# Attention of the first block: V products over four units, padded q and k, and the steps at the edges of the attention

## The chip, the cores and the metric

One core of a Trainium2 chip runs the whole program in one launch. The metric is the device time of a run in microseconds (us), as the median of several runs; lower is better.

## The reference, cut to what matters

The program computes two blocks one after the other on a sequence of 1024 positions with width 1024, in float32: the first block (two layers, l = 0 and 1), then a hybrid layer. Only the first block is touched.

```python
for l in range(2):
    h = rms_norm(x, norm_g[l]);  p = h @ w_in[l]
    c_q, c_kv, k_pe, z_a, u_f, z_f, g_a, g_f = split(p)
    q = rms_norm(rms_norm(c_q) @ w_uq)      # 8 heads of 96: 64 plain, 32 rotary
    k, v = ...                              # k: 8 heads of 96, v: 8 heads of 64
    rope(q[..., 64:]), rope(k[..., 64:])
    o_a = softmax(q @ k.T * 96 ** -0.5) @ v # 1024 x 1024 scores per head
    y_a = (o_a * silu(z_a)) @ w_attn_proj[l]
    y_f = (fourier(u_f) * silu(z_f)) @ w_fourier_proj[l]
    m = sigmoid(g_a + b0) * y_a + sigmoid(g_f + b1) * y_f
    x = x + m @ w_out[l]
```

## The kernel before, in words

Every engine runs a list of instructions written by hand, with semaphores between the engines. The eight PSUM banks (128 x 512 float32) are handed over by the counters `full[b]` (written by TensorE) and `free[b]` (read by the others); `begin(b)` waits for a bank, `arrive(b)` waits for its content.

**Attention.** A *unit* is one head and one tile of 128 queries: 64 units per layer, u = 8h + t. For a unit TensorE makes the scores (`scores`, L551: q and k are kept as a rounded part and a rest, so 3 products for each half of the 1024 keys, 6 matmuls of 512 columns, 96 rows deep), into the bank pair 0/1 or 2/3. VectorE takes the row maximum (L1712), ScalarE the exponential (L1295). TensorE turns the probabilities (`p_turn`, L561: 8 transposes of 128x128 into banks 4 and 5); VectorE copies both banks for an even unit (L1720, L1721), for an odd one VectorE copies bank 4 (L1725) and ScalarE bank 5 (L1288), into one of two buffers `PT`. `pv_pair` (L575) multiplies two turned units with V at once: V has 64 columns, so the even unit stands in the left column half of the array and the odd unit in the right one, 8 steps of keys with 128 columns moved for each. After eight units VectorE copies the head's output from bank 6 (`head_out`, L1687 and L1688).

On TensorE step u is: scores of u+1, for even u the V products of units u-2 and u-1, a turn of q or k for the next head if one is due (`qk_turn`, L535, four for each head, all through bank 7), the turn of unit u. GpSimd stages q and k of each head beforehand (L2174 to L2188). Each turned quarter is copied and rounded by ScalarE (`qk_copy`, L1271), and its rest is made by VectorE (`qk_rest`, L1695), which frees the bank. The four turns of head 0 go through bank 7 one after the other before the first scores.

**Around the last head.** In the last head's steps 1 to 4 ScalarE also rounds a quarter of h (`round_h`, L1275) and VectorE makes its rest (`rest_of_h`, L1700); a step later ScalarE rounds h in place (`in_place`, L1279). When the last head's output is copied, VectorE sets `s_o`. Then follow weights and rests 0 and 1, h parts 4 to 7 (ScalarE, VectorE; parts 6 and 7 in place by GpSimd, L2195), the turn of the row sums (L597) and its copy (L1323). Then TensorE runs *unit weights* c = 0 to 7 with n = 0, 1 (`unit`, L614, L617, L620: 24 matmuls of 512 columns each, over k = 0 to 7). Before it starts, ScalarE has rounded weight 0 into `wHi` (`round_weights`, L1311) and VectorE has its rest (`rest`, L1737).

**End of a layer.** For each m = 0 to 7 the gates (`unit`) and the two projections (L644), which VectorE multiplies and adds to `mT` (L1772, L1774). Then `m @ w_out` (L658, L661, L664) needs the rounded m (ScalarE L1356 and L1363), its rest (`m_rest`, L1779) and the rounded weights with their rest (L1360, `w_out_rest` L1785).

**SyncE's queue** loads the weights in chunks into two slots; a load waits for `w_used[slot]`. Slot 0's chunk "zf" (unit weights 0 to 3) waits for the first Fourier matmul; "za" in slot 1 waits for `s_o`.

## Time and profile before

| | us |
|---|---|
| median of 3 runs | 2679.63 (2676.92 to 2685.85) |
| the profiled execution's own time | 2685.18 |
| its span, first to last instruction | 2683.4 |
| TensorE busy | 2534.9 (94%) |
| VectorE busy | 1365.2 (51%) |
| ScalarE busy | 797.5 (30%) |
| GpSimd busy | 367.4 (14%) |
| mean granted TensorE clock | 0.974 of full |

PE is TensorE's matmuls, PEld its weight loads, DVE VectorE, ACT ScalarE, POOL GpSimd. The span is cut into stretches by time from its start; a granted clock of 1.00 is 2.4 GHz, 0.50 is 1.2 GHz. Attention of layer 0 runs from 212 to 459 us, of layer 1 from 1130 to 1377 us. A float32 matmul leaves two records, a float32 transpose and a rounded matmul one.

### The profile page before, as it was taken

How to read it: one execution, taken by the hardware profiler on the slowest of the kernel's cores; microseconds unless marked ns; L12 is line 12 of the kernel's file. 1: busy time of each engine (PE TensorE's matmuls, PEld its weight loads, DVE VectorE, ACT ScalarE, POOL GpSimd, SP SyncE). 2: the span in 40 equal slices, each digit the busy share in tenths (PEclk: the TensorE clock that was granted, in tenths of full speed). 3: DMA queues.
4: the chain of work that ended last, by engine and by line, in shares of the span. 5: the costliest groups of instructions: out<-in, count | busy, mean ns of one | idle time of the engine just before them, and what ended most of it. 6: DMA issues, size and time to landing. Idle time of an engine off the chain costs nothing.

```text
span 2683.4 us, 30039 instructions
## 1 busy us (share of the span) xinstructions
PE 2534.9 (94%) x12173; PEld 1776.7 (66%) x12173; DVE 1365.2 (51%) x2206; ACT 797.5 (30%) x1434; POOL 367.4 (14%) x477
## 2 busy tenths in 40 slices
PE   7998997999999999899979999999999998989997
PEld 5856886876666787588868666667556544445553
DVE  2255776221113243467753111133689999955763
ACT  3343545111113142345441111131351113143341
POOL 0023320000000001233100000000234672100000
PEclk9998999999999999999989999999999999999998
DMA  5010000211113121000020111122111011020000
GB/s 197 29 47 1 1 1 32 58 47 42 30 47 126 35 93 44 32 1 1 1 64 24 48 47 47 55 94 69 66 39 34 1 41 40 32 71 24 32 16 32
DMA packets 106377, 116.78 MB, mean 44 GB/s; under 512 B 20704, under 2 KB 78784, under 8 KB 106240
## 3 DMA queue, kind: packets, MB, share of 16 engines
q1 hardware_dynamic: 105088, 110.66, 13.4%
q10 hardware_dynamic: 1152, 4.19, 0.4%
q8 instruction: 97, 1.59, 0.2%
q14 instruction: 40, 0.33, 0.0%
HBM read 96.82 MB, written 16.84 MB: 42 GB/s over the span
## 4 chain that ended last, share of the span: by engine, by line
PE 84%; DVE 8%; ACT 4%; issue 1%; POOL 1%; SPq 1%; DMA 1%; DVEq 0%; POOLq 0%; ACTq 0%
PE PS L644 8%; PE PS L614 7%; PE PS L617 7%; PE PS L620 7%; PE PS L551 6%; PE PS L445 4%; PE PS L561 4%; PE PS L575 4%; PE PS L969 4%; PE PS L735 4%; PE PS L882 2%; PE PS L658 2%; PE PS L661 2%; PE PS L664 2%; PE PS L940 2%; PE PS L490 2%
## 5 line engine op out<-in xcount | busy, mean ns | idle before, releaser
L614 PE MATMUL PS<-hHi,R2bR 128*128 128x512 f32 x768 | 306.7, 399 | 15.4 <-ACT rows L1323 15.4
L617 PE MATMUL PS<-hLo,R2bR 128*128 128x512 f32 x768 | 300.5, 391 | 0.0
L620 PE MATMUL PS<-hHi,R2bR 128*128 128x512 f32 x768 | 300.2, 391 | 0.0
L1737 DVE TENSOR_TENSOR R2bR<-W,R2bR 128x1024 fp32r<-128x1024 f32 x48 | 57.5, 1222 | 309.2 <-ACT R2bR L1311 309.2
L1343 ACT ACTIVATE R3a<-PS,pT 128x512 f32<-128x512 f32 x64 | 42.3, 687 | 467.5 <-PE PS L620 467.5
L614 PEld LDWEIGHTS PS<-hHi,R2bR 128*128 128x128 f32 x768 | 145.2, 189 | 48.9 <-ACT rows L1323 15.7
L1712 DVE TENSOR_REDUCE negm<-PS 128x1 f32<-128x1024 f32 x128 | 156.6, 1223 | 29.8 <-PE PS L551 25.1
L617 PEld LDWEIGHTS PS<-hLo,R2bR 128*128 128x128 f32 x768 | 145.3, 189 | 33.0 <-issue 3.3
L735 PE MATMUL PS<-hT,W 128*128 128x512 f32 x384 | 166.6, 595 | 0.0
L1295 ACT ACTIVATE R2b<-PS,negm 128x1024 f32<-128x1024 f32 x128 | 142.4, 1112 | 78.8 <-DVE negm L1712 78.8
L620 PEld LDWEIGHTS PS<-hHi,R2bR 128*128 128x128 f32 x768 | 145.2, 189 | 30.5
L561 PE MATMUL PS<-ident,R2b 128*128 128x128 f32 x1024 | 138.6, 279 | 5.6 <-ACT R2b L1295 3.8
L2012 DVE MAX8 ssc<-R2a 128x8 f32<-128x384 f32 (+4 forms) x160 | 132.4, 828 | 5.4
L575 PE MATMUL PS<-R2b,R 128*64 128x128 f32 x2048 | 129.1, 280 | 6.4 <-DVE R2b L1725 3.1
L575 PEld LDWEIGHTS PS<-R2b,R 128*64 128x64 f32 x2048 | 113.7, 139 | 29.5 <-issue 22.3
L735 PEld LDWEIGHTS PS<-hT,W 128*128 128x128 f32 x384 | 72.9, 191 | 91.0 <-issue 90.9
L2013 DVE MATCH_REPLACE8 R2a<-ssc,R2a 128x384 f32<-128x384 f32 (+4 forms) x160 | 129.4, 809 | 0.0
L561 PEld LDWEIGHTS PS<-ident,R2b 128*128 128x128 f32 x1024 | 113.8, 142 | 20.8 <-issue 13.1
L1772 DVE TENSOR_TENSOR R3a<-R3a,PS 128x512 f32<-128x512 f32 x64 | 43.8, 684 | 162.7 <-PE PS L644 162.7
L445 PE MATMUL PS<-W,hT 128*128 128x256 f32 (+1 forms) x512 | 119.8, 393 | 0.9 <-DMA W<-in_w_in 0.7
L969 PE MATMUL PS<-W,R 128*128 128x512 f32 x256 | 117.2, 603 | 0.8 <-DVE R L2060 0.8
L551 PE MATMUL PS<-R3aR 96*128 96x512 f32 x256 | 114.8, 448 | 3.1 <-DVE WR L1695 3.1
(354 smaller groups left out, 4645.8 us busy)
## 6 DMA issues: line engine op xcount, KB each, us to landing
W<-in_w_in SPq DMA_DIRECT2D x10, 2048.0 KB, 8.5
W<-in_w_in SPq DMA_DIRECT2D x33, 512.0 KB, 4.7
xres<-R SPq DMA_DIRECT2D x3, 4096.0 KB, 18.7
W<-in_w_out SPq DMA_DIRECT2D x6, 2048.0 KB, 7.9
R<-xres SPq DMA_DIRECT2D x2, 4096.0 KB, 19.0
R<-in_x ACTq DMA_DIRECT2D x8, 512.0 KB, 8.2
W<-in_w_in SPq DMA_DIRECT2D x4, 1024.0 KB, 6.8
R3a<-rsums SPq DMA_DIRECT2D x16, 256.0 KB, 5.4
```

Source lines behind the costliest of these rows:

```text
L445: mm = pe.matmul(o[:, 0:hi - lo], hT[:, k, t * P:(t + 1) * P], wc[:, k, lo:hi], start=(k == 0), stop=(k == 7))
L551: mm = pe.matmul(PS[:, b + n, :], x[0:QK, t * P:(t + 1) * P], y[0:QK, n * 512:(n + 1) * 512], start=(i == 0), stop=(i == 2))
L561: mm = pe.transpose(o[:, k * P:(k + 1) * P], Pb[u % 2][:, c * P:(c + 1) * P], ident[:, :])
L575: mm = pe.matmul(PS[e * VD:(e + 1) * VD, 6, at_], v_tok[:, k, h, :], PT[e][:, k * P:(k + 1) * P], start=(k == 0), stop=(k == 7))
L614: mm = pe.matmul(o, wHi[c % 2][:, k, :], hHi[:, k, ns], start=(k == 0), stop=False)
L617: mm = pe.matmul(o, wHi[c % 2][:, k, :], hLo[:, k, ns], start=False, stop=False)
L620: mm = pe.matmul(o, wLo[c % 2][:, k, :], hHi[:, k, ns], start=False, stop=(k == 7))
L644: mm = pe.matmul(o, g[:, k0 + k, :], rhs[:, k, n * 512:(n + 1) * 512], start=(k == 0), stop=(k == 3))
L735: mm = pe.matmul(o, wz[:, k, m * P:(m + 1) * P], xT[:, k, n * 512:(n + 1) * 512], start=(k == 0), stop=(k == 7))
L969: mm = pe.matmul(o, mix[:, k, t * P:(t + 1) * P], wo[:, k, :], start=(k == 0), stop=(k == 7))
L1295: act.activation(Pb[u % 2], PS[:, b:b + 2, :].rearrange("p a c -> p (a c)"), ACT.Exp, bias=negm[:, u:u + 1], accum_out=rsum[:, u:u + 1]).t ...
L1712: dve.tensor_reduce(negm[:, u:u + 1], PS[:, b:b + 2, :].rearrange("p a c -> p (a c)"), AX.X, ALU.max, negate=True).then_inc(s_nm, 1)
```

## The change

1. V products of four units at once (`pv_quad`): each column half takes two units, 256 columns moved. Eight key steps, cut into pieces of 3, 3 and 2 in TensorE's steps 4q+4, 4q+5, 4q+6; the last quad in one piece.
2. Six buffers `PT` (three pairs): one pair as before, two in weight slot 0, and for the last head's units in the place of `q_tok`. Slot 0 is now given to "zf" by the V product that ends head 6; copies for the last head wait for `s_stage`.
3. q and k padded from 96 to 128 columns with zeros (a memset by GpSimd), so turns, copies and scores use 128 rows.
4. The four turns of head 0 use banks 4, 5, 6, 7.
5. `head_out` moves from step 1 to step 3 of the next head.
6. Around the last head: weight 0 is rounded in step 63, its rest comes before the last `head_out`; unit 0 starts right after the last V product, k = 0 to 3 for both n first, then k = 4 to 7; the row sums are turned behind it, into bank 7, and copied after ScalarE's second SiLU.
7. End of a layer: `m_rest` and `w_out_rest` of k = 0, 1 come before VectorE's multiplications of m = 7.

```diff
+def turn_bank(h, i):
+    return 4 + i if h == 0 else 7
...
-        PT = [R2b[:, 2, :], R2b[:, 3, :]]
+        def PT_pair(u):
+            i = u // 2 % 3
+            if i == 0:
+                return R2b[:, 2:4, :]
+            home = W[:, 0, 0:4096] if u < UNITS - NT else r0[:, 0:4096]
+            return home[:, (i - 1) * 2048:i * 2048].rearrange("p (a c) -> p a c", a=2)
+        def PT(u):
+            return PT_pair(u)[:, u % 2, :]
...
                 def scores(u):
...
                     if t == 0:
-                        pe.wait_ge(free[7], bk.count(7))
+                        for i in range(4):
+                            if h == 0 or i == 3:
+                                pe.wait_ge(free[4 + i], bk.count(4 + i))
...
-                            mm = pe.matmul(PS[:, b + n, :], x[0:QK, t * P:(t + 1) * P],
-                                           y[0:QK, n * 512:(n + 1) * 512], start=(i == 0), stop=(i == 2))
+                            mm = pe.matmul(PS[:, b + n, :], x[:, t * P:(t + 1) * P],
+                                           y[:, n * 512:(n + 1) * 512], start=(i == 0), stop=(i == 2))
...
+                def pv_quad(q, part):
+                    h, a_ = q // 2, q % 2
+                    if part[0] == 0:
+                        if a_ == 0:
+                            begin(6)
+                        pe.wait_ge(free[4], pt_count[4 * q + 3][0])
+                        pe.wait_ge(free[5], pt_count[4 * q + 3][1])
+                    for k in part:
+                        for e in range(2):
+                            mm = pe.matmul(PS[e * VD:(e + 1) * VD, 6, 2 * a_ * P:2 * (a_ + 1) * P], v_tok[:, k, h, :],
+                                           PT_pair(4 * q + 2 * e)[:, :, k * P:(k + 1) * P],
+                                           start=(k == 0), stop=(k == 7))
+                            if (h, a_, k, e) == (H - 2, 1, NT - 1, 0):
+                                mm.then_inc(w_used[0], 1)
...
-                    if u >= 2 and u % 2 == 0:
-                        pv_pair(u - 1)
+                    if u == UNITS:
+                        pv_quad(u // 4 - 1, range(NT))
+                    elif u >= 4 and u % 4 < 3:
+                        pv_quad(u // 4 - 1, range(3 * (u % 4), min(NT, 3 * (u % 4) + 3)))
...
-                pe.wait_ge(s_o, l + 1)
-                o = begin(0)
-                pe.transpose(o[:, 0:P], sums[:, :], ident[:, :]).then_inc(full[0], 1)
...
-                for c in range(8):
+                o = [begin(0), begin(1)]
+                for n in range(2):
+                    unit(0, n, o[n], None, range(KD // 2))
+                for n in range(2):
+                    unit(0, n, o[n], None, range(KD // 2, KD)).then_inc(full[n], 1)
+                pe.wait_ge(s_o, l + 1)
+                o = begin(7)
+                pe.transpose(o[:, 0:P], sums[:, :], ident[:, :]).then_inc(full[7], 1)
+                for c in range(1, 8):
...
@@ ScalarE @@
+                    if u == UNITS - 1:
+                        act.wait_ge(full[5], bk.count(5))
+                        round_weights(0)
...
+                for k in range(4, KD):
+                    round_h(k)
+                in_place(4)
                 act.wait_ge(s_o, l + 1)
...
                 round_weights(1)
...
+                in_place(5)
...
@@ VectorE @@
+                dve.wait_ge(full[5], bk.count(5))
                 rest(0)
...
+                head_out(H - 1)
+                dve.wait_ge(free[6], bk.count(6))
+                dve.memset(mark[:, :], 0.0).then_inc(s_o, 1)
+                for k in range(4, KD):
+                    rest_of_h(k)
                 rest(1)
...
                 for m in range(KD):
                     if m + 1 < KD:
                         rest(8 + 2 * m + 2)
                         rest(8 + 2 * m + 3)
+                    else:
+                        for k in range(2):
+                            m_rest(k)
+                            w_out_rest(k)
...
@@ GpSimd @@
+                pool.memset(stage[:, :, :, QK:P], 0.0)
```

The order of the instructions before and after, at three places. First TensorE in the middle of the attention, from the turn of an even unit on, before (L551 scores, L561 turn of probabilities, L575 V products, L535 turn of q or k):

```order
L561 MATMUL PS<-ident,R2b 128x128 x8
L551 MATMUL PS<-R3aR 128x512
L551 MATMUL PS<-WR,R3aR 128x512
L551 MATMUL PS<-R3aR,WR 128x512
L551 MATMUL PS<-R3aR 128x512
L551 MATMUL PS<-WR,R3aR 128x512
L551 MATMUL PS<-R3aR,WR 128x512
L535 MATMUL PS<-ident,R 96x128 x4
L561 MATMUL PS<-ident,R2b 128x128 x8
```

and in the changed kernel the first piece of a quad, with the turn behind it (L566 scores, L576 turn of probabilities, L590 V products):

```order
L566 MATMUL PS<-R3aR,WR 128x512
L590 MATMUL PS<-R2b,R 64x256
L590 MATMUL PS<-W,R 64x256
L590 MATMUL PS<-R2b,R 64x256
L590 MATMUL PS<-W,R 64x256
L590 MATMUL PS<-R2b,R 64x256
L590 MATMUL PS<-W,R 64x256
L576 MATMUL PS<-ident,R2b 128x128 x8
```

Where one group of 16 matmuls of 128 columns stood in every second step, groups of 6, 6 and 4 matmuls of 256 columns stand in three of four steps. Second, VectorE at the end of the attention (L1737 rest of a unit weight, L1700 rest of h, L1732 the mark that sets `s_o`), before:

```order
L1725 COPY R2b<-PS 128x512
L1684 RECIPROCAL sums<-sums 128x8
L1687 COPY R2a<-PS 64x4x128
L1688 COPY R2a<-PS 64x4x128
L1732 MEMSET mark 128x1
L1737 TENSOR_TENSOR R2bR<-W,R2bR 128x1024
L1700 TENSOR_TENSOR hLo<-hT,R3aR 128x1024 x2
L1737 TENSOR_TENSOR R2bR<-W,R2bR 128x1024
L1700 TENSOR_TENSOR hLo<-hT,R3aR 128x1024 x2
```

and after:

```order
L1754 COPY R2b<-PS 128x512
L1762 TENSOR_TENSOR R2bR<-W,R2bR 128x1024
L1710 RECIPROCAL sums<-sums 128x8
L1713 COPY R2a<-PS 64x2x256
L1714 COPY R2a<-PS 64x2x256
L1768 MEMSET mark 128x1
L1727 TENSOR_TENSOR hLo<-hT,R3aR 128x1024 x4
L1762 TENSOR_TENSOR R2bR<-W,R2bR 128x1024
```

The rest of weight 0 now stands ahead of the last head's output. Third, VectorE at the end of a layer (L1790 is `m_rest`, L1796 `w_out_rest`, L1813 and L1815 the multiplications and the addition), after:

```order
L1790 TENSOR_TENSOR hHi<-R,R3aR 128x1024
L1796 TENSOR_TENSOR R2bR<-W,R2bR 128x512
L1790 TENSOR_TENSOR hHi<-R,R3aR 128x1024
L1796 TENSOR_TENSOR R2bR<-W,R2bR 128x512
L1813 TENSOR_TENSOR R3a<-R3a,PS 128x512 x2
L1815 TENSOR_TENSOR R<-R3a 128x512
L1813 TENSOR_TENSOR R3a<-R3a,PS 128x512 x2
L1815 TENSOR_TENSOR R<-R3a 128x512
```

Before, the first four of these stood behind the last four.

## Rows read from the trace of the kernel before

**Rows 1.** The page: TensorE's busy time, and the chain by engine.
```profile
PE 2534.9 (94%) x12173; PEld 1776.7 (66%) x12173; DVE 1365.2 (51%) x2206; ACT 797.5 (30%) x1434; POOL 367.4 (14%) x477
...
PE 84%; DVE 8%; ACT 4%; issue 1%; POOL 1%; SPq 1%; DMA 1%; DVEq 0%; POOLq 0%; ACTq 0%
```

**Rows 2.** Stretches: length, busy (records) of PE, PEld, DVE, ACT, POOL; PEclk, DMA, GB/s.
```profile
212.20:222.30 10.10, 3.80 (x17) 2.35 (x17) 2.75 (x4) 3.29 (x5) 6.43 (x9) 0.59 0.00 0
222.30:231.20 8.90, 8.90 (x24) 6.89 (x25) 3.74 (x4) 2.77 (x5) 2.39 (x3) 0.50 0.01 2
231.30:424.30 193.00, 192.29 (x1751) 163.91 (x1749) 143.87 (x183) 96.12 (x165) 53.56 (x66) 1.00 0.01 1
459.40:468.90 9.50, 0.33 (x1) 0.14 (x1) 8.23 (x9) 7.96 (x9) 0.98 (x1) 0.70 0.63 221
469.00:473.50 4.50, 4.50 (x11) 3.53 (x12) 0.00 (x0) 1.28 (x1) 4.50 (x2) 0.50 0.31 92
842.50:846.30 3.80, 0.00 (x0) 0.01 (x1) 3.11 (x4) 1.13 (x2) 0.00 (x0) 0.91 0.00 0
846.40:852.40 6.00, 6.00 (x14) 4.68 (x15) 3.66 (x4) 4.45 (x6) 0.00 (x0) 0.50 0.63 230
```

**Rows 3.** The chain in the steady attention (start, length in us, what).
```profile
300.69 1.02 PE PS L561 x8
...
303.54 0.87 PE PS L561 x8
304.41 1.38 PE PS L551 x6
305.79 1.90 PE PS L575 x32
```

**Rows 4.** The chain from the Fourier matmuls through head 0's turns.
```profile
209.36 0.88 PE PS L526 x4
...
212.10 0.14 issue
...
214.42 1.07 PE PS L535 x4
...
215.51 0.60 ACT R3aR L1271
...
216.21 0.70 DVE WR L1695
...
222.29 0.77 PE PS L551
```

**Rows 5.** The chain in the last head, one step of 5.53 us.
```profile
435.66 1.15 DVE negm L1712
...
441.19 1.15 DVE negm L1712
```

**Rows 6.** Timeline around the end of the attention: VectorE, GpSimd.
```profile
459.36 0.69 DVE L1687 COPY R2a<-PS 64x512 f32<-64x512 f32 x1 [2.48 <-PE PS L575]
466.62 2.35 DVE L1700 TENSOR_TENSOR hLo<-hT,R3aR 128x1024 fp32r<-128x1024 f32 x2
467.92 5.60 POOL L2195 TENSOR_TENSOR hHi<-hT,hLo 128x1024 fp32r<-128x1024 f32 x2 [77.16 <-DVE hLo L1700]
```

**Rows 7.** Timeline, TensorE: start of unit 1, and the 42nd matmul behind it.
```profile
482.09 0.39 PE L614 MATMUL PS<-hHi,R2bR 128*128 128x512 f32 x1
...
491.61 0.39 PE L614 MATMUL PS<-hHi,R2bR 128*128 128x512 f32 x1
```

**Rows 8.** Timeline, end of the layer: rounding of m, its first rest.
```profile
829.35 1.05 ACT L1356 ACTIVATE R3aR<-R 128x1024 fp32r<-128x1024 f32 x1
839.16 0.69 DVE L1772 TENSOR_TENSOR R3a<-R3a,PS 128x512 f32<-128x512 f32 x1 [6.21 <-PE PS L644]
843.92 1.22 DVE L1779 TENSOR_TENSOR hHi<-R,R3aR 128x1024 fp32r<-128x1024 f32 x1
```

**Rows 9.** Issues of DMAs, 455 to 600 us: size, time to landing.
```profile
W<-in_w_in SPq DMA_DIRECT2D x1, 2048.0 KB, 8.2
```

More of the change, by code:

```diff
@@ L531, in qk_turn @@
                     pe.wait_ge(s_stage, l * 2 * H + 2 * h + i // 2 + 1)
-                    o = begin(7)
+                    b = turn_bank(h, i)
+                    o = begin(b)
                     for j in range(4):
                         t = 4 * (i % 2) + j
-                        mm = pe.transpose(o[0:QK, j * P:(j + 1) * P], stage[:, i // 2, t, :], ident[:, :])
+                        mm = pe.transpose(o[:, j * P:(j + 1) * P], stage[:, i // 2, t, :], ident[:, :])
                         if h == i == j == 0:
                             mm.then_inc(w_used[1], 1)
-                    mm.then_inc(full[7], 1)
+                    mm.then_inc(full[b], 1)
                 def scores(u):
@@ L563, in p_turn @@
                     pt_count.append((bk.count(4), bk.count(5)))
-                def pv_pair(u):
-                    h, t = u // NT, u % NT
-                    if t == 1:
-                        begin(6)
-                    pe.wait_ge(free[4], pt_count[u][0])
-                    pe.wait_ge(free[5], pt_count[u][1])
-                    at_ = slice((t // 2) * P, (t // 2 + 1) * P)
-                    for k in range(NT):
-                        for e in range(2):
-                            mm = pe.matmul(PS[e * VD:(e + 1) * VD, 6, at_], v_tok[:, k, h, :],
-                                           PT[e][:, k * P:(k + 1) * P], start=(k == 0), stop=(k == 7))
-                    if t == NT - 1:
+                def pv_quad(q, part):
[6 more added lines that the diff above has]
+                    for k in part:
+                        for e in range(2):
+                            mm = pe.matmul(PS[e * VD:(e + 1) * VD, 6, 2 * a_ * P:2 * (a_ + 1) * P], v_tok[:, k, h, :],
[3 more added lines that the diff above has]
+                                mm.then_inc(w_used[0], 1)
+                    if a_ == 1 and part[-1] == NT - 1:
                         mm.then_inc(full[6], 1)
@@ L592, in _, with unit @@
                         p_turn(u)
-                pe.wait_ge(s_o, l + 1)
-                o = begin(0)
-                pe.transpose(o[:, 0:P], sums[:, :], ident[:, :]).then_inc(full[0], 1)
                 def follows(c):
                     return 0 < c <= 8 or c % 2 == 1
-                def unit(c, n, o, last_used=None):
+                def unit(c, n, o, last_used=None, part=range(KD)):
                     ns = slice(n * 512, (n + 1) * 512)
-                    if n == 0:
+                    if n == part[0] == 0:
                         pe.wait_ge(s_wlo, l * N_SPLIT + c + 1)
-                    for k in range(KD):
+                    for k in part:
                         if c == n == 0:
@@ L1334, in _ @@
                         round_weights(i // 2 + 2)
+                    if i == 1:
+                        o = arrive(7)
+                        act.activation(rsT, o[UNITS:P, 0:P], ACT.Copy).then_inc(free[7], 1)
+                        act.wait_ge(s_hlo, l * KD + KD)
+                        act.wait_ge(free[7], bk.count(7))
+                        act.sem_inc(s_rsT, 1)
                 for m in range(KD):
@@ L1724, in _ @@
                             o = arrive(4)
[L1725 removed]
+                            dve.tensor_copy(PT(u - 1)[:, 0:512], o).then_inc(free[4], 1)
                     if u - 1 in QK_TURNS:
@@ L1729, in _ @@
                         rest_of_h(u % NT - 1)
-                head_out(H - 1)
-                dve.wait_ge(free[6], bk.count(6))
-                dve.memset(mark[:, :], 0.0).then_inc(s_o, 1)
                 def rest(c):
@@ L2171, in _ @@
                     rk = rsh[:, 1, :, h:h + 1]
-                    if h >= 1:
+                    if h == 1:
+                        pool.wait_ge(full[4], bk.count(4))
+                        pool.wait_ge(full[5], bk.count(5))
+                    elif h >= 2:
                         pool.wait_ge(full[7], bk.count(7) - 2)
@@ L2181, in _ @@
                     pool.tensor_tensor(x2p, rtp[:, 2], rtp[:, 3], ALU.add).then_inc(s_stage, 1)
+                    if h == 1:
+                        pool.wait_ge(full[6], bk.count(6))
                     if h >= 1:
@@ L2189, in _ @@
                                        ).then_inc(s_stage, 1)
-                    for _ in range(4):
-                        bk.take(7)
+                    for i in range(4):
+                        bk.take(turn_bank(h, i))
                 for k in range(H_ACT, KD):
@@ L2198, in _ @@
                     if b != 7:
-                        bk.n[b] += n
+                        bk.n[b] += n - (b > 3)
+                bk.take(7)
                 for n in ROUND[7:]:
```

86 lines of the change are left out of this document (36 added, 50 removed).

## The prediction

> **What bounds the kernel now.** I read the page first: TensorE is busy for 94% of the span and makes 84% of the chain that ended last [rows 1]. So a change pays where it shortens TensorE's stream, fills its idle stretches, or brings its clock back. The busy time by stretches says where that can be [rows 2]. In the steady attention (231.3 to 424.3 us) TensorE is busy for 192.29 of 193.0 us at clock 1.00: only its own work counts there. Four stretches of layer 0 are different. In 212.2 to 222.3 it is busy for 3.8 of 10.1 us, and 222.3 to 231.2 runs wholly at clock 0.50. In 459.4 to 468.9 it does next to nothing, and 469.0 to 473.5 runs at 0.50. In 842.5 to 846.3 it does nothing, and 846.4 to 852.4 runs at 0.50. Layer 1's chain has the same pieces with the same lengths, 918 us later. The chains and timelines show what ends each wait.
>
> **Part by part, for one layer.** I count gains as positive.
>
> *Turns of head 0 in four banks.* Now each turn waits until VectorE has taken the rest of the one before: turn 1.07, copy 0.60, rest 0.70 and latencies make a round of 2.62 us [rows 4], four of them from 212.24 to 222.29. TensorE is free at 210.24, when the last Fourier matmul ends, and VectorE frees the last Fourier bank (7) at 212.10 [rows 4]. Banks 4 to 6 are free earlier, so three turns run from 210.3 on and the fourth at 212.24, where the first stands now. Its copy ends near 213.5. VectorE is the last: four rests of 0.6 to 0.7 from 212.1 on end near 214.6, and the scores start near 214.7 instead of 222.29. **+7.6.** It can't be much less (four rests in line is all that is left) nor more (bank 7): 6.8 to 7.8. GpSimd may stage head 1 from about 211.3 on; its memset of the padding comes before head 0's staging, which is done 10 us before the first turn, so it costs nothing.
>
> *Clock at the start.* After work became dense at 222.3 the clock stayed at 0.50 for 8.9 us; at the two other places dense work got it back after 4.6 us and 6.1 us [rows 2]. I expect it to fall again (TensorE has about 2 us of idle before the scores), and to come back after some 6 to 7 us: half of the 2 us fewer, **+1.0**, between 0 (the same 8.9 us) and 2.2 (4.6 us).
>
> *V products.* Two units of 128 columns take 1.90 us [rows 3]. A transpose moves 128 columns in 0.87/8 = 0.109 us [rows 3], and 16 pairs of V records, the halves side by side, would take 16 x 0.109 = 1.74. So the columns already stream at full rate in both halves, and 0.16 us is paid on entering. Behind them the 8 transposes take 1.02 instead of 0.87 [rows 3]: another 0.15 on leaving. A group of V products therefore costs 0.31 us beside its columns. 256 columns take 0.88/4 = 0.22 (by L526) [rows 4], so a quad streams in about 3.47 us against 3.49 for two pairs: nothing. But a quad has three groups where two pairs had two. Per layer there are 15 x 3 + 1 = 46 groups instead of 32, 14 more, 4.3 us. Not all of it is paid. Through heads 1 to 6 it is: 12 quads x (0.31 - 0.02) = 3.5 us. The first quad starts two steps later than the first pair, so the last head begins with one pair (2.05 with its edges) owed. In the last head the steps 57 to 60 take 5.53 us each [rows 5], set by a loop over VectorE (rest of h, maximum) and ScalarE (exponential, two roundings), which TensorE waits for; a group more is hidden there. At the end the last quad is whole, 3.78 in place of 2.05, and the group at step 62 is shorter (1.18 for 2.05); `head_out` goes out of the loop into a wait of VectorE in step 59, which gives back little, since TensorE's group at step 57 stands there. Sum: the last V product ends 3.5 - 2.05 + 1.73 - 0.87 = 2.3 later, less a few tenths for `head_out`: **-2.0**, between -1 and -4.3.
>
> The Trainium skill (TensorEngine Tiling (Array Packing), Key Properties) says that changing the tiling mode drains the engine, which speaks against cutting a quad into three. The row above agrees with it (0.31 us beside the columns), and by it every one of the 14 groups would pay.
>
> *Padding.* Six score matmuls of 96 rows take 1.38 us [rows 3]; unit matmuls of 128 rows take (491.61 - 482.09)/42 = 0.227 us, 1.36 for six [rows 7]. If the 0.02 us is the 96 rows, 64 units give up to 1.5 us a layer; if it is the entry from the transposes, nothing. **+0.7**, 0 to 1.5.
>
> The Trainium skill (TensorE: Matmul & The Clock Gate, "Why this matters for your kernels") has a matmul with few rows take as long as one with 128; by that this term is 0 and the total 44.0 instead of 45.4.
>
> *End of the attention.* Now VectorE's copy behind TensorE's last V product starts at 459.36; two copies, the mark, weight 0, four roundings and the turn of the sums stand between it and unit 0 at 468.9, which runs at 0.50 to 473.5 and ends where unit 1 begins, 482.09 [rows 2, 6, 7]: 22.7 us. In the new order weight 0 is rounded in step 63 and its rest follows, both before the last V product, so unit 0 starts at once (T'). Parts k = 0 to 3 for both n take 24 x 0.227 = 5.45 us. Meanwhile VectorE copies the output (2 x 0.69), marks (T' + 1.5), and makes four rests, 2.35 for two [rows 6]: parts 4 to 7 at T' + 2.7, 3.8, 5.0, 6.1. ScalarE follows for 4 and 5. GpSimd needs 2.8 us each for 6 and 7 [rows 6]: T' + 7.8 and 10.6. TensorE wants part 6 at T' + 6.8 and part 7 at 7.5, so it waits about 3 us in all, finishes n = 0 at 11.3 and n = 1 at 14.0; the turn of the sums adds 0.2. **+8.5** (22.7 - 14.2), between 6.5 (GpSimd slower beside VectorE, or the clock falling in the wait) and 11 (no wait at all: 22.7 - 10.9 - 0.2 = 11.6).
>
> What is queued there: on ScalarE step 63's weight stands before the copy of bank 5, for which the last V product waits; it fits into the wait for that turn. It also needs chunk "zf", which SyncE now issues only after step 58's V product (near 432 in today's trace) and which lands 8.2 us later [rows 9]; it is wanted near 454, so 14 us are left. Behind it on SyncE stand only loads that wait for `s_o` anyway. The sums go to DRAM some 17 us behind T' instead of 10, and are first multiplied in at 521.
>
> *End of the layer.* VectorE now starts the first rest of m at 843.92, after all of m = 7, though ScalarE had rounded m at 829.35 to 830.4 [rows 8]. In the new order the four moved operations (two of 1.23, two of 0.69) and ScalarE's part run from 830.4 to about 836, before the projection that ends the wait of 6.21 us at 839.16 [rows 8], so the multiplications aren't late. TensorE goes on at 842.5 instead of 846.3: 3.8 us [rows 2]; and without that gap the clock should not fall, which gives back half of 6.1 us. **+6.9**, between 4 (the clock falls nevertheless) and 7. Parts 2 to 7 follow every 3.3 us, TensorE needs 5.45 for each.
>
> **Sum**: 7.6 + 1.0 - 2.0 + 0.7 + 8.5 + 6.9 = 22.7 us a layer, 45.4 for two. The profiled execution took 2685.18 us, 5.5 above the median, so it would take 2639.8; against the median of 2679.63 it is 2634.2. The ends of the terms give 2 x 13.0 = 26 and 2 x 28.5 = 57 us, thus 2623 to 2654.
>
> **The rivals.**
>
> *The clock stays low (chance 0.10).* Dense work from 214.7 on could run at 0.50 until 231.2 as now, 16.5 us instead of 8.9, which costs 3.8; and the 3 us wait in unit 0 could make the clock fall, for 4.5 us as at 469 [rows 2], which costs 2.3. With the 1.0 not gained: 7.1 us a layer, 2648. For it: the clock fell at all three gaps. Against it: TensorE works before and after these waits, and does so for much less than half of them now.
>
> *VectorE becomes late in the attention (0.07).* The shortest step (no V products) has 1.38 + 0.44 + 0.87 = 2.7 us of TensorE, and with `head_out` VectorE has 1.15 + 1.6 + 1.2 = 3.9 in it. If the delay isn't caught up in the next, longer steps, each head loses about 1 us, 14 in all: 2648. Against it: VectorE is busy for only 143.87 of 193 us [rows 2].
>
> *The two column halves don't overlap with 256 columns (0.05).* The moved operand is now a two-piece pattern over two buffers, in two memory regions. If the halves ran one after the other, each of the 64 pairs of units would stream for 3.49 instead of 1.74 us: +112 us, 2746, slower than before. The change comes out slower from the point where 45.4/112 = 41% of the overlap is lost. Against it: the two records of a pair start side by side now, also from different buffers, which is why 32 take 1.90 us [rows 3].
>
> *More than forecast (0.06).* No fall of the clock at the start (3 more), no wait in unit 0 (3), full padding gain (0.8): 6.8 a layer, 2620.
>
> **How the numbers follow.** The forecast has 0.72 and is 2634. With the first, second and last rival near its ends, 2619 to 2653 leaves out less than 2 in 10. About 0.3% (8 us) is what a measurement of this kernel can tell from no change. Faster by more: forecast, clock, late VectorE, the better case and a sliver of the third rival, 0.94. Within it 0.02. Slower 0.04.
>
> **What would show it.** Right: first scores 2.5 us behind the last Fourier matmul's VectorE operations; the V products in groups of about 1.3, 1.3 and 0.87 us with 0.3 beside them, and 28.5 instead of 28.0 us for a head; unit 0 directly behind the last V product, GpSimd the releaser of a 2 to 3 us wait within it; w_out directly behind the projections at clock 1.00. Wrong: V groups of 2.6 us; a wait for ScalarE's weight 0 or for its DMA; VectorE as releaser of TensorE in the steady steps; clock 0.50 for more than 9 us behind the first scores.

## The result, and the profile after

| | before | changed |
|---|---|---|
| median of four runs, us | 2679.60 (2676.92 to 2685.85) | 2647.86 (2641.66 to 2649.50) |
| the profiled execution's own time | 2685.18 | 2641.66 |
| its span | 2683.4 | 2639.6 |
| mean granted TensorE clock | 0.974 | 0.988 |

The changed kernel is faster: the ratio of the mean times is 0.9874, with an interval of 0.985 to 0.9898, and the medians differ by 31.7 us. The forecast was 45.4. A second set of runs of the changed kernel (e14, below) has a median of 2645.92 and the same ratio, 0.9874 (0.9861 to 0.9888).

The two profiled executions lie at opposite ends: the one of before is 5.5 us above its median, the one of after 6.2 below. So the spans differ by 43.8 us where the medians differ by 31.7, and a sum over the spans has to be cut into stages. The *touched stages* reach from the end of the first Fourier part to the end of the first block. They took 1645.2 us before, 1606.4 after, and 1609.2 in the profile of the second set, whose execution (2649.58) lies above its median, as that of before does. The change is thus worth 36.0 to 38.8 us in its own stages, and 36.0 where two executions at like ends are compared. The rest of the difference between the spans lies in code that the change doesn't touch. The kernel before reached the end of the Fourier part 1.8 us sooner (210.2 us against 212.0), and took 6.8 us more behind the first block, where the clock's spells (stretches in which it is at 0.50) lie elsewhere.

The page of the changed kernel, for [rows 1]: busy times, and the chain by engine.

```profile
PE 2519.7 (95%) x11149; PEld 1714.2 (65%) x11149; DVE 1368.2 (52%) x2206; ACT 797.1 (30%) x1434; POOL 370.1 (14%) x479
...
PE 85%; DVE 8%; ACT 3%; POOL 2%; issue 1%; SPq 1%; DMA 1%; DVEq 0%; POOLq 0%; ACTq 0%
```

TensorE has 1024 matmul records fewer (two records for each of 512 V matmuls saved), and its busy time fell by only 15.2 us: about two thirds of the 43.8 us between the spans is idle time closed.

Stretches of the changed kernel, for [rows 2] (length, then busy time and records of PE, PEld, DVE, ACT, POOL; PEclk, DMA share, GB/s):

```profile
212.00:216.30 4.30, 1.92 (x16) 1.47 (x14) 3.80 (x8) 3.58 (x6) 3.23 (x2) 1.00 0.00 0
216.40:225.00 8.60, 7.42 (x42) 6.14 (x43) 5.66 (x7) 3.77 (x8) 5.56 (x9) 1.00 0.01 2
242.20:413.70 171.50, 171.50 (x1153) 125.64 (x1152) 126.86 (x162) 83.74 (x145) 44.53 (x55) 1.00 0.00 1
455.00:471.80 16.80, 13.13 (x50) 10.04 (x50) 10.00 (x9) 4.84 (x5) 6.56 (x2) 0.90 0.37 125
832.30:838.30 6.00, 6.00 (x28) 4.94 (x28) 4.38 (x6) 2.54 (x4) 0.00 (x0) 1.00 0.75 265
```

The gap at the start is 4.3 us instead of 12, and the clock behind it is 1.00. The steady attention is full of TensorE's work, as before. The end of the attention, 16.8 us long, is no longer idle at its start but is not full: 13.13 us busy, at clock 0.90. w_out runs at 1.00 from its first matmul.

The same stages measured from matmul to matmul, in us. "First scores" counts from the last Fourier matmul, "end of attention" from the last V product to unit 1, "gap" from the last projection to w_out.

| layer 0 / layer 1 | before | changed |
|---|---|---|
| first scores | 12.07 / 12.08 | 4.41 / 4.40 |
| head 0 | 30.18 / 30.24 | 25.75 / 26.78 |
| heads 1 to 6 | 168.00 / 168.00 | 171.61 / 171.61 |
| head 7 to the last V product | 38.85 / 38.85 | 41.27 / 39.59 |
| end of attention | 22.77 / 22.84 | 16.80 / 16.72 |
| gap before w_out | 3.87 / 3.88 | -0.56 / -0.56 |
| w_out | 90.18 / 90.19 | 87.62 / 87.62 |

Everything between unit 1 and the gap has the same length to 0.2 us.

The chain in the steady attention of the changed kernel, for [rows 3] (start, length, what; L566 scores, L576 turn, L590 V products, L548 turn of q or k):

```profile
326.07 1.01 PE PS L590 x8
327.09 1.02 PE PS L576 x8
328.11 1.39 PE PS L566 x6
329.50 0.44 PE PS L548 x4
329.94 0.87 PE PS L576 x8
330.81 1.39 PE PS L566 x6
332.19 1.45 PE PS L590 x12
333.64 1.02 PE PS L576 x8
```

The piece of a quad with 6 matmuls (12 records) takes 1.45 us and that with 4 takes 1.01; every one has a turn of 1.02 us behind it, where the turn with no V products ahead takes 0.87.

The start of the attention in the timeline, for [rows 4] (start, length, engine, line, what; in brackets the idle time ahead and its releaser):

```profile
211.81 1.47 PE L548 MATMUL PS<-ident,R 128*128 128x128 f32 x12
213.76 2.47 DVE L1722 TENSOR_TENSOR WR<-PS,R3aR 128x512 fp32r<-128x512 f32 x4
216.38 0.47 PE L566 MATMUL PS<-R3aR 128*128 128x512 f32 x1 [1.76 <-DVE WR L1722]
```

Three turns run at once, VectorE's four rests stand in line, the scores follow. And the end of the attention, for [rows 6, 7]: VectorE, then GpSimd, then the start of unit 1.

```profile
455.04 0.69 DVE L1713 COPY R2a<-PS 64x512 f32<-64x512 f32 x1 [4.74 <-PE PS L590]
457.62 3.49 DVE L1727 TENSOR_TENSOR hLo<-hT,R3aR 128x1024 fp32r<-128x1024 f32 x3
461.02 3.38 DVE L1762 TENSOR_TENSOR R2bR<-W,R2bR 128x1024 fp32r<-128x1024 f32 x1
460.05 6.56 POOL L2232 TENSOR_TENSOR hHi<-hT,hLo 128x1024 fp32r<-128x1024 f32 x2 [75.79 <-DVE hLo L1727]
471.81 0.48 PE L630 MATMUL PS<-hHi,R2bR 128*128 128x512 f32 x1
```

TensorE's waits in that stretch (line waited for: us in total, times, longest):

```profile
PE PS L630 <- POOL hHi L2232: 3.7, 2, 2.3
```

Unit 0 starts at 454.94 and waits twice, for GpSimd's parts 6 and 7. GpSimd took 3.28 and 3.32 us for them, and VectorE's rest of weight 1 (L1762), which runs beside it, 3.38 us.

### The profile page after: what moved, and what is told of

It reads as the page before. It is cut to its first block, busy times and chain, and to the rows that moved or that the text cites. A ratio compares the mean times of both kernels' runs of the same rounds, so it can differ in the third digit from the quotient of the medians.

```text
span 2639.6 us, 27983 instructions
## 1 busy us (share of the span) xinstructions
PE 2519.7 (95%) x11149; PEld 1714.2 (65%) x11149; DVE 1368.2 (52%) x2206; ACT 797.1 (30%) x1434; POOL 370.1 (14%) x479
## 4 chain that ended last, share of the span: by engine, by line
PE 85%; DVE 8%; ACT 3%; POOL 2%; issue 1%; SPq 1%; DMA 1%; DVEq 0%; POOLq 0%; ACTq 0%
PE PS L668 8%; PE PS L630 6%; PE PS L636 6%; PE PS L633 6%; PE PS L566 6%; PE PS L459 5%; PE PS L590 4%; PE PS L576 4%; PE PS L993 4%; PE PS L759 4%; PE PS L906 2%; PE PS L964 2%; PE PS L685 2%; PE PS L504 2%; PE PS L688 2%; PE PS L682 2%
## 5 line engine op out<-in xcount | busy, mean ns | idle before, releaser
L1762 DVE TENSOR_TENSOR R2bR<-W,R2bR 128x1024 fp32r<-128x1024 f32 x48 | 61.8, 1311 | 307.2 <-ACT R2bR L1309 307.2
L576 PE MATMUL PS<-ident,R2b 128*128 128x128 f32 x1024 | 137.7, 277 | 11.7 <-DVE R L1749 8.6
L576 PEld LDWEIGHTS PS<-ident,R2b 128*128 128x128 f32 x1024 | 112.0, 140 | 40.2 <-issue 23.9
L566 PE MATMUL PS<-R3aR 128*128 128x512 f32 x256 | 112.4, 439 | 3.5 <-DVE WR L1722 3.5
L590 PE MATMUL PS<-W,R 128*64 128x256 f32 x576 | 114.8, 389 | 0.0
L668 PE MATMUL PS<-R3b,W 128*128 128x512 f32 x256 | 112.5, 592 | 0.0
L668 PE MATMUL PS<-R2a,W 128*128 128x512 f32 x256 | 112.4, 592 | 0.0
```

Source lines behind the costliest of these rows:

```text
L566: mm = pe.matmul(PS[:, b + n, :], x[:, t * P:(t + 1) * P], y[:, n * 512:(n + 1) * 512], start=(i == 0), stop=(i == 2))
L576: mm = pe.transpose(o[:, k * P:(k + 1) * P], Pb[u % 2][:, c * P:(c + 1) * P], ident[:, :])
L590: mm = pe.matmul(PS[e * VD:(e + 1) * VD, 6, 2 * a_ * P:2 * (a_ + 1) * P], v_tok[:, k, h, :], PT_pair(4 * q + 2 * e)[:, :, k * P:(k + 1) * ...
L668: mm = pe.matmul(o, g[:, k0 + k, :], rhs[:, k, n * 512:(n + 1) * 512], start=(k == 0), stop=(k == 3))
```

## The experiments

All are edits of the changed kernel. One number besides the median is given for each, the length of the touched stages in its profile (1645.2 before; 1606.4 and 1609.2 in the two profiles of the changed kernel), since the rest of the program adds a few us of its own from run to run. Ratios are of mean times, to the kernel before, run beside it.

### The V products

Two pieces of four key steps instead of 3, 3 and 2 (e3_two_pieces):

```diff
-                    elif u >= 4 and u % 4 < 3:
-                        pv_quad(u // 4 - 1, range(3 * (u % 4), min(NT, 3 * (u % 4) + 3)))
+                    elif u >= 4 and u % 2 == 0:
+                        pv_quad(u // 4 - 1, range(4 * (u % 4 // 2), 4 * (u % 4 // 2) + 4))
```

> The changed kernel, but with each quad's V products in two groups of four key steps (steps 4q+4 and 4q+6) instead of three groups of 3, 3 and 2. Theory (each group costs 0.31 us beside its columns, whatever its length): heads 1 to 6 take 171.6 - 12 x 0.31 = 167.9 us instead of 171.6 in each layer, the whole run is 7 us faster than the changed kernel, 2641. Rival (the loss of 0.6 us a head comes from VectorE being late in the short steps, which longer groups make worse): heads 1 to 6 stay at 171 us or more, and TensorE's turns show waits for VectorE.

2641.06 us (2638.93 to 2642.21), ratio 0.9848 (0.9831 to 0.9864); touched stages 1601.6. Heads 1 to 6 take 168.16 us in both layers instead of 171.61. The chain of its profile (start, length, what):

```profile
328.98 1.40 PE PS L566 x6
330.38 1.88 PE PS L590 x16
332.25 1.02 PE PS L576 x8
```

16 records of 256 columns take 1.88 us, as 32 of 128 did [rows 3]. Twelve groups fewer in the six heads save 3.45 us, 0.29 for a group. So 3.45 of the 3.61 us that the quads lost in these heads is the third group; the padding has the rest (below). In the last head, where VectorE and ScalarE set the pace, two pieces are 0.6 us a layer slower (40.2 us in both layers of e10 against 39.6 in both of e5, which differs from it in the pieces alone).

Pairs of 128 columns as before the change, all other parts kept (e6_pairs):

```diff
...
-                    if u == UNITS:
-                        pv_quad(u // 4 - 1, range(NT))
-                    elif u >= 4 and u % 4 < 3:
-                        pv_quad(u // 4 - 1, range(3 * (u % 4), min(NT, 3 * (u % 4) + 3)))
+                    if u >= 2 and u % 2 == 0:
+                        pv_pair(u - 1)
...
```

> The changed kernel with V products in pairs of units as before (128 columns in each half, 32 groups a layer), everything else as changed, the six buffers too. Theory (four units at once bring nothing, the groups cost): heads 1 to 6 take 168.0 us as in the kernel before, the last V product comes 4 to 6 us earlier behind the first scores than in the changed kernel (238.6 and 238.0 us there), and the run is 8 to 11 us faster, near 2638. Rival (256 columns save weight loads, or six buffers without quads bring waits): heads 1 to 6 at 170 us or more, the run no faster than 2645.

2700.98 us (2700.30 to 2702.88), ratio 1.0074 (1.0059 to 1.0089): slower than before, a miss. Heads 1 to 6 took 193.18 us. Here are TensorE's waits from 240 to 440 us, and one of them in the chain:

```profile
PE PS L590 <- DVE R2a L1711: 16.6, 6, 2.9
```

```profile
286.91 1.23 DVE negm L1736
288.13 0.11 DVE sums L1707
...
288.27 0.69 DVE R2a L1710
288.96 0.01 issue
288.97 0.71 DVE R2a L1711
289.68 0.04 issue
289.72 2.56 PE PS L590 x32
292.28 1.90 PE PS L576 x8
```

I had kept one part of the change that only quads can bear. `head_out` stands in VectorE's step 3, but the first pair of the next head wants bank 6 in TensorE's step 2, so six times TensorE waits 2.8 us, and five times the clock falls behind the wait (the V products and the turn above take 2.56 and 1.90 us instead of 1.90 and 1.02). 16.6 + 5 x 1.7 = 25.1 is the whole of what it lost against the 168.0 us of before. So the run says nothing of pairs. The next one does, with the output copied in step 1 as before (e9_pairs_out_in_step_1):

```diff
-                    if u >= NT and u % NT == 3:
+                    if u >= NT and u % NT == 1:
                         head_out(u // NT - 1)
```

> The pairs once more, with head_out back in step 1 of the next head as in the kernel before. Theory (the run with pairs lost its 25 us in each layer only to bank 6, which the next head's first pair wants in step 2 while head_out stands in step 3): heads 1 to 6 take 168.0 us, the last V product comes about 4 us earlier behind the first scores than in the changed kernel, the run takes 2637 to 2642, 6 to 11 us less than the changed kernel. Rival (the six buffers or the places in other tiles cost something themselves): heads 1 to 6 at 170 us or more.

2641.32 us (2638.21 to 2642.77), ratio 0.9845 (0.983 to 0.986); touched stages 1604.1. Heads 1 to 6 take 168.64 us, 0.6 more than expected; the padding accounts for 0.2 of that (e2), and the rest is open. Its steady stretch, to be held against the third line of the changed kernel's above:

```profile
242.20:413.70 171.50, 171.50 (x1559) 146.29 (x1556) 128.16 (x165) 84.85 (x146) 44.70 (x55) 1.00 0.01 1
```

Pairs cost 20.65 us more of weight loads here, and TensorE's matmuls fill the stretch in both: the loads ran beside them anyway. By the medians quads in two pieces (2641.06) and pairs (2641.32) take the same time; quads in three pieces are slower by their extra groups. The quad itself, the part with which the change began, is worth nothing that a median shows, and at most 0.5 us a layer in heads 1 to 6.

### Padding

The slices of 96 rows back in turns, copies, rests and scores (e2_rows96):

```diff
...
-    mm = pe.matmul(PS[:, b + n, :], x[:, t * P:(t + 1) * P],
-                   y[:, n * 512:(n + 1) * 512], start=(i == 0), stop=(i == 2))
+    mm = pe.matmul(PS[:, b + n, :], x[0:QK, t * P:(t + 1) * P],
+                   y[0:QK, n * 512:(n + 1) * 512], start=(i == 0), stop=(i == 2))
...
```

> The changed kernel with q and k at 96 rows again (turns, copies, rests and scores), without the memset. Theory (padding brings nothing): heads 1 to 6 stay at 171.6 us within 0.2, the run within 2 us of the changed kernel, 2646 to 2650. Rival (the forecast's 0.7 us a layer is there and hidden by something else): heads 1 to 6 take 172.3 us or more.

2646.12 us (2643.85 to 2648.99), ratio 0.9869 (0.9854 to 0.9884); touched stages 1609.8. Heads 1 to 6 take 171.40 us with 96 rows and 171.61 with 128. The two kernels can't be told apart by the median, and by the stage 96 rows are no slower. The 0.02 us of a unit's scores beyond six plain matmuls is not the rows, since the scores with 128 rows take 1.39 us in the chain above. That it is the entry from the transposes is the reading left over; no run tests it.

### The turns of head 0

All four through bank 7 again (e1_bank7):

```diff
 def turn_bank(h, i):
-    return 4 + i if h == 0 else 7
+    return 7
```

> The changed kernel with head 0's four turns through bank 7 again, one after the other. Theory (the turns are worth 7.7 us a layer, and the clock that doesn't fall 1.5 to 2.5 more): first scores 12.1 us behind the last Fourier matmul instead of 4.4, clock at 0.50 over the first scores again for 7 us or more, the run 18 to 22 us slower than the changed kernel, near 2667. Rival (the clock is a matter of chance and not of these waits): 15 us slower, near 2663, with clock 1.00 over the first scores in one of the layers.

2660.89 us (2659.99 to 2662.86), ratio 0.992 (0.9906 to 0.9935); touched stages 1621.9. The first scores come 12.23 and 12.19 us behind the Fourier part instead of 4.41: the 7.8 us are shown. The part behind them is not as I had it. Its stretches:

```profile
212.00:224.00 12.00, 3.92 (x17) 2.60 (x17) 4.19 (x8) 3.51 (x6) 6.51 (x9) 0.59 0.00 0
224.00:234.00 10.00, 9.36 (x42) 7.57 (x43) 5.76 (x7) 4.08 (x8) 2.31 (x3) 0.80 0.01 2
```

The scores start at 223.99. With the same turns as the kernel before, the clock is back at 228.0, some 4 us later, and not after 8.9 us [rows 2]; in layer 1 it is back 5.5 us behind the first scores. Head 0 took 27.05 us. In the changed kernel it took 25.75 and 26.78, and 25.75 and 27.03 in the second profile. So the clock's part of this edit is between nothing and 1.3 us a layer.

### The end of the attention

ScalarE rounds parts 6 and 7 of h in place, and GpSimd has nothing there (e5_act_rounds_all):

```diff
-H_ACT = 6
+H_ACT = 8
...
-                in_place(5)
+                for k in range(5, KD):
+                    in_place(k)
```

> The changed kernel with h parts 6 and 7 rounded in place by ScalarE (behind part 5) instead of GpSimd. Theory (GpSimd, slowed by VectorE's rest of weight 1 beside it and slowing it, sets the end of unit 0): unit 0 takes 11.0 to 11.6 us instead of 16.8, VectorE's rest of weight 1 takes 1.2 us instead of 3.4, the run is 10 to 12 us faster than the changed kernel, near 2637. Rival (VectorE's rests of h or the clock set it): unit 0 still takes 14 us or more.

2634.17 us (2633.03 to 2635.06), ratio 0.9824 (0.9809 to 0.9838); touched stages 1595.1. Last V product to unit 1 is 11.20 us in both layers, for 16.80 and 16.72. From its timeline, ScalarE and VectorE, and from its chain the last quad with the start of unit 0:

```profile
458.25 2.94 ACT L1303 ACTIVATE hHi<-hT 128x1024 fp32r<-128x1024 f32 x3
459.62 1.22 DVE L1763 TENSOR_TENSOR R2bR<-W,R2bR 128x1024 fp32r<-128x1024 f32 x1
```

```profile
449.93 3.67 PE PS L590 x32
453.60 0.43 PE PS L630
454.03 0.23 PE PS L633
```

ScalarE needs 0.98 us for each part, TensorE never waits, the clock doesn't fall, and the same operation of VectorE takes 1.22 us where it took 3.38 beside GpSimd.

The turn of the sums ahead of unit 0, with GpSimd (e8_sums_first) and with ScalarE's rounding (e13_act_sums_first):

```diff
+                pe.wait_ge(s_o, l + 1)
+                o7 = begin(7)
+                pe.transpose(o7[:, 0:P], sums[:, :], ident[:, :]).then_inc(full[7], 1)
                 o = [begin(0), begin(1)]
...
-                pe.wait_ge(s_o, l + 1)
-                o = begin(7)
-                pe.transpose(o[:, 0:P], sums[:, :], ident[:, :]).then_inc(full[7], 1)
```

> The changed kernel, but TensorE waits for s_o and turns the sums before unit 0 instead of behind it. Theory (unit 0's end hangs on GpSimd's rounding of parts 6 and 7, so an early start of its first half buys only what is left over): unit 0 starts 1.7 us later, unit 1 starts at the same time within 0.5 us, the run the same as the changed kernel within 2 us. Rival (TensorE's own start sets it): unit 1 starts 1.7 us later in each layer, the run 3.4 us slower.

2639.22 us (2637.68 to 2644.37), ratio 0.9842 (0.9827 to 0.9857); touched stages 1604.8. Its waits from 450 to 475 us:

```profile
PE PS L630 <- POOL hHi L2232: 2.1, 1, 2.1
PE PS L641 <- DVE mark L1768: 1.6, 1, 1.6
```

Unit 0 starts 1.9 us later, and the two waits for GpSimd, 3.7 us together, become one for the mark and one for GpSimd, with the same sum. From the last V product to unit 2 it is 27.70 us against 27.79 in layer 0, and 26.11 against 27.71 in layer 1, where the clock didn't fall in this execution. So while GpSimd makes parts 6 and 7, starting unit 0 at once buys nothing. The 6 us a layer that the change gains here would then come from the rest of its item 6 (the new order on VectorE and ScalarE, and unit 0 in two halves over k). No run undoes that part, and its gain is read from the stages alone. The median is some 7 us lower than the changed kernel's two. The touched stages account for 1.6 to 4.4 us of that, which is the clock in layer 1; the rest I can't explain, and 7 us is less than what a measurement can tell.

> The changed kernel with parts 6 and 7 rounded by ScalarE and with the wait for s_o and the turn of the sums ahead of unit 0. Theory (without GpSimd's part TensorE itself sets the end of unit 0, so its early start now counts): unit 1 starts 1.0 to 1.8 us later behind the last V product than with ScalarE's rounding alone (12.5 to 13.1 instead of 11.2), the run 2 to 4 us slower than that, near 2637. Rival (the early start buys nothing in any case): unit 1 at 11.3 to 11.6, no difference.

2633.87 us (2631.58 to 2638.26), ratio 0.9832 (0.9818 to 0.9845); touched stages 1597.5 against 1595.1 of e5. With GpSimd out of the way the order counts: last V product to unit 1 is 12.80 us against 11.20, 1.6 us a layer. The two medians, of different sessions, don't show it: 3 us in 2634 is within their spread.

### The end of the layer

The first rests of m and of w_out back behind all multiplications (e7_m_rest_back):

```diff
-                    else:
-                        for k in range(2):
-                            m_rest(k)
-                            w_out_rest(k)
...
-                for k in range(2, KD):
+                for k in range(KD):
```

> The changed kernel with the rests of m and of w_out for k = 0, 1 behind the multiplications of m = 7 again. Theory: TensorE idles 3.9 us between the projections and w_out, and w_out takes 90.2 instead of 87.6 us because of the clock: 7.0 us a layer, the run 14 us slower than the changed kernel, near 2662. Rival (the clock would have fallen in some other place anyway): 4.4 us a layer, near 2657.

2657.20 us (2655.92 to 2659.59), ratio 0.9907 (0.989 to 0.9923); touched stages 1620.8, 11.6 to 14.4 above the changed kernel. The gap is 3.88 us again in both layers, and w_out takes 88.91 and 90.07 us instead of 87.62. This is the chain in its layer 0. The clock shows in the length of a matmul, 0.43 us at 0.50 and 0.23 at 1.00:

```profile
834.68 0.75 PE PS L682
835.44 0.43 PE PS L685
...
838.34 0.23 PE PS L688
```

The spell took 3.4 us here and 6.8 in layer 1, where its first microsecond lay in the gap. Gap (4.4 us more than in the changed kernel, where w_out starts 0.56 before the projections' last record ends) and clock together are 5.7 and 6.9 us, the gap being the same in both layers.

### Best parts together

Two combinations ran side by side with the changed kernel without an edit (e14_changed_again): two pieces and ScalarE's rounding (e10_two_pieces_act, the edits of e3 and e5), and pairs with the output in step 1 and ScalarE's rounding (e11_pairs_act, the edits of e6, e9 and e5).

> The changed kernel once more, on the chip of the next three. From its stages in the first profile (38.7 us saved in the first block, and nothing of the change behind it) both theories give 2641 to 2648; it is the measure for the runs beside it.

> The changed kernel with V products in two groups for a quad, and h parts 6 and 7 rounded by ScalarE. Theory (the two effects are independent): 3.5 us a layer from the groups and 5.5 from unit 0, 18 us less than the changed kernel, 2626 to 2630. Rival (unit 0's new end only moves waits to the weights behind it, or the clock takes part of it back): 2632 or more.

> As the run before, but with V products in pairs and head_out in step 1, so no quads at all. Theory: the same time as with two groups for a quad, within 2 us (same number of groups, last V product shorter by 1.7 us, one pair more before head 1): 2625 to 2630. Rival (256 columns are worth something after all): 4 us or more behind the two groups.

| | median (range), us | ratio to before (interval) | touched stages |
|---|---|---|---|
| e14_changed_again | 2645.92 (2644.46 to 2649.58) | 0.9874 (0.9861 to 0.9888) | 1609.2 |
| e10_two_pieces_act | 2627.75 (2622.89 to 2632.31) | 0.9804 (0.9791 to 0.9818) | 1587.4 |
| e11_pairs_act | 2630.12 (2627.32 to 2633.84) | 0.9814 (0.9801 to 0.9828) | 1591.4 |

The two small edits of e10 give 18.2 us beyond the changed kernel, as expected, and 53 us against the kernel before. Its chain behind the last quad (3.67 us, at full clock, as expected of 8 matmuls of 256 columns in each half):

```profile
445.11 3.67 PE PS L590 x32
448.79 0.43 PE PS L630
```

Pairs in the place of quads (e11) are 2.4 us off, less than these medians can tell.

## Why the prediction was right, and where its terms were off

The range held and so did the sign; the forecast of 2634.2 was 13.7 us low. In us a layer, by the stages of the two profiles:

| term | forecast | layer 0 | layer 1 |
|---|---|---|---|
| turns of head 0 | +7.6 | +7.7 | +7.7 |
| clock at the start | +1.0 | +2.4 | +1.4 |
| V products and padding | -1.3 | -4.0 | -2.3 |
| end of attention | +8.5 | +6.0 | +6.1 |
| end of the layer | +6.9 | +7.0 | +7.0 |
| sum (of unrounded rows) | 22.7 | 19.0 | 19.9 |

The misses partly cancel. V products, padding and the end of the attention fall short by 8.6 us over both layers, and the clock at the start, which differed from layer to layer (below), gives 1.8 back. That part of the agreement is luck.

The first two rows divide the stages "first scores" and "head 0", from whose gain of 4.4 and 3.5 us in head 0 the pair that is owed to the next head (2.05 us) is taken off and put into the third row.

*Turns of head 0.* Right, to 0.1 us. The order that I gave (three turns at once, bank 7 last, four rests in line) is the one in the timeline, 2 us later throughout in this profile since the start of the program was. e1 undoes it and gets 7.8 back.

*Clock at the start.* In layer 0 the clock did not fall at all over the first scores, in layer 1 for 3.4 us. The sign was right, but the step behind the size, that the turns set how long the clock stays low, falls with e1: with the old turns it was low over the scores for 4.0 and 5.5 us, where the profile of before has 8.9 and 9.1. Of the gain in head 0 one part is the change's and another that of the execution, and these profiles don't divide it. The price was off too. I had put the case without any fall at 3 us more than the forecast (last rival); in layer 0 it came, and gave 1.4 more. At full clock TensorE, which had been busy for 29.47 of head 0's 30.18 us, is busy for 23.89 of 25.75, and waits 1.2 us for ScalarE's first exponential.

*V products.* The mechanism was right and its main step exact: heads 1 to 6 lost 3.6 us where the sum had 3.5, and e3 shows that it is the third group. In the last head I expected that a loop over VectorE and ScalarE would hide groups, and it did: its steps are 5.53 us long as before [rows 5]. The end of it was mis-sized by the clock: the last quad in layer 0 took 5.38 us (chain, below) where e5 and e10 have 3.67, since it ran at 0.50 for 3.4 us. In layer 1, without that spell, the row is 2.3, against the 2.0 forecast for the V products.

```profile
449.65 5.38 PE PS L590 x32
455.04 0.69 DVE R2a L1713
```

The Trainium skill (TensorEngine Tiling (Array Packing), Key Properties) has the engine drain when the tiling mode changes. The trace and e3 agree, with a price of 0.29 to 0.31 us for each group of V products.

*Padding.* I chose +0.7 between 0 and 1.5; e2 shows no gain, and 0.2 us lost in heads 1 to 6. The Trainium skill (TensorE: Matmul & The Clock Gate, "Why this matters for your kernels") has a matmul with few rows take as long as one with 128. It was the better guide: e2 agrees with it (171.40 against 171.61 us).

*End of the attention.* The term that was mis-sized most over both layers, 8.5 for 6.0. The step that failed is "GpSimd needs 2.8 us each for 6 and 7 [rows 6]". The 2.8 is half of a merged row of two operations, 5.60 us, and the two are not alike. Taken one by one, with VectorE's rest beside the first, they are, in the kernel before:

```profile
467.76 1.22 DVE L1700 TENSOR_TENSOR hLo<-hT,R3aR 128x1024 fp32r<-128x1024 f32 x1
467.92 3.28 POOL L2195 TENSOR_TENSOR hHi<-hT,hLo 128x1024 fp32r<-128x1024 f32 x1 [77.16 <-DVE hLo L1700]
471.16 2.36 POOL L2195 TENSOR_TENSOR hHi<-hT,hLo 128x1024 fp32r<-128x1024 f32 x1
```

So 3.28 is the time beside VectorE and 2.36 the time alone. In the changed kernel both have VectorE beside them:

```profile
459.89 1.22 DVE L1727 TENSOR_TENSOR hLo<-hT,R3aR 128x1024 fp32r<-128x1024 f32 x1
460.05 3.28 POOL L2232 TENSOR_TENSOR hHi<-hT,hLo 128x1024 fp32r<-128x1024 f32 x1 [75.79 <-DVE hLo L1727]
463.29 3.32 POOL L2232 TENSOR_TENSOR hHi<-hT,hLo 128x1024 fp32r<-128x1024 f32 x1
```

GpSimd began when I said (5.04 us behind the last V product, forecast 5.0), but the second part came at 11.6 and not at 10.6. TensorE's waits were 3.7 us for the forecast's 3. The clock then fell for 3.4 us at the end of unit 0, in both layers, which costs 1.7. This is the mechanism of my first rival, which had put it at 2.3. 1.0 + 1.7 accounts for the 2.5 that are missing. In the second profile of the same kernel the spell took 6.8 us in both layers and the stretch 17.55 and 17.87 us, so the price of the clock varies here by about 1 us. I had named "GpSimd slower beside VectorE" as the lower bound of the term, but costed the second part's share of it at nothing in the sum. e5 confirms it: with GpSimd idle the wait, the slower VectorE and the fall of the clock all go, and the stretch is 5.6 us shorter. Moving VectorE's rest of weight 1 behind GpSimd's parts instead was not tried.

*End of the layer.* Right, to 0.1 us; e7 undoes it and loses 4.4 us by the gap and 1.3 to 2.5 us by the clock.

*The sum.* 38.9 of 45.4 us by the two profiles, less 0.1 a layer behind unit 1; 36.0 by the profile of the second set. That one is the fairer: its execution, like the profiled one of before, is at the slow end of its kernel's runs, and the medians measured side by side in that session (2680.97 and 2645.92) differ by 35.1. The forecast had carried the distance of the profiled execution to its median over as a constant, 5.5 us. In this kernel it was between -6.2 and +3.7. Of the four runs of the changed kernel in the first set the fastest has the highest clock, 0.988 against 0.984 to 0.985 in the others; so this part of the miss (what lies between 36 to 39 and the 31.7 of the medians) is, as far as these runs show, the scatter of executions and not a term of the change.

*The rivals.* "The clock stays low" happened in its second half, the wait in unit 0. "VectorE becomes late" did not: the steady stretch is full of TensorE. Its mechanism showed in e6 though, where `head_out` in the wrong step cost 25 us a layer. "The two column halves don't overlap" is refuted: 16 records of 256 columns take 1.88 us, as 32 of 128 did (1.90).

## What to carry to other kernels

Count the groups, not only the columns: where TensorE changes between whole-array and column-tiled work, each visit had a fixed price here, so larger tiles pay only if the visits become fewer, and cutting them up to spread the work can cost more than they bring. Weight loads that already run beside the matmuls are no gain when they go. Look at the operations of a merged row one by one before you divide it: the mean of 3.28 and 2.36 hid the very effect that was to come. When an engine is given the last operations on a path that another engine works beside, price both from a stretch in which they overlap, and ask whether a third engine is free; here moving two roundings from GpSimd to ScalarE was worth more than cutting the quads in two (11 to 14 us against 5 to 8 in the touched stages).

## What the runs showed of the hardware that I had not expected

GpSimd and VectorE slowed each other. GpSimd's operation on 128x1024 took 2.36 us alone and 3.28 to 3.32 with VectorE's operation beside a part of it, and VectorE's rest of weight 1 took 3.38 us beside GpSimd and 1.22 without it (e5). The ends of the operations suggest how. In the changed kernel VectorE's last rest of h ends at 461.11, and GpSimd's first part 2.22 us later, at 463.33. VectorE's rest of weight 1, though it starts at 461.02, ends 1.07 us after that, at 464.40, and GpSimd's second part 2.21 us after that, at 466.61. In the kernel before GpSimd's first part ends 2.22 us behind VectorE's rest (468.98 and 471.20). Each time the later one ends about its own full time behind the earlier one, so they look like operations that take turns, each as a whole, and don't share. This also accounts for the rest of h, which started first and was not slowed. It is a reading of starts and ends, which repeat in both layers and in every profile where GpSimd makes these parts; the profile's spans of GpSimd are rough, and no run varied the order. The Trainium skill (GPSIMD Engine Reference, Key points) says that GpSimd shares its SBUF interfaces with VectorE and contends with VectorE instructions that have two SBUF inputs. The rests of h and of a weight are such instructions, and the trace agrees.

The clock's spells at 0.50 are no fixed property of a kernel. They took from 3.4 to 17.1 us, and in the touched stages most of them lie near stretches in which TensorE had waited. From one execution of the changed kernel to the next, the spell in layer 0's last head is at 433.0 for 3.4 us and at 434.4 for 6.8, that of unit 0 at 467.2 for 3.4 and at 465.1 for 6.8. Over layer 0's first scores there is none, over layer 1's there is one. So in this kernel a term for the clock could be forecast at best in sign, and its size varied by a factor of two between executions.
